# Delta-rule stage of a transformer kernel: two directions in lockstep, or as two streams eight steps apart

## The reference, cut to what matters

```python
def gdn_chunked(q, k, v, log_a, beta, s0):
    ...
    a_mat = jnp.where(strict, jnp.einsum('bhnid,bhnjd->bhnij', kb, k) * decay, 0.0) + jnp.eye(C, dtype=F32)
    rhs = jnp.concatenate([v * beta, kb * jnp.exp(g)[..., None]], axis=-1)
    sol = lax.linalg.triangular_solve(a_mat, rhs, left_side=True, lower=True)
    u, w = sol[..., :DV], sol[..., DV:]
    ...
    def step(s, xs):
        qk_c, qd_c, w_c, u_c, ke_c, ge_c = xs
        v_new = u_c - jnp.einsum('bhcd,bhdv->bhcv', w_c, s)
        o = jnp.einsum('bhcd,bhdv->bhcv', qd_c, s) + jnp.einsum('bhcs,bhsv->bhcv', qk_c, v_new)
        s = s * ge_c[..., None, None] + jnp.einsum('bhcd,bhcv->bhdv', ke_c, v_new)
        return s, o

def bidir_scan(scan_fn, ctx_f, ctx_b, lat_f, lat_b, s0):
    o_cf, s_f = scan_fn(*ctx_f, s0)
    o_cb, s_b = scan_fn(*flip_seq(ctx_b), s0)
    o_lf, _ = scan_fn(*lat_f, s_f)
    o_lb, _ = scan_fn(*flip_seq(lat_b), s_b)
    return o_lf + jnp.flip(o_lb, axis=2), (o_cf, o_cb)
```

## Time and profile before

| what | us |
|---|---|
| median of 3 runs (2361.44 to 2371.91) | 2362.75 |
| the profiled execution, its own time | 2375.91 |
| the profiled execution, span of the trace | 2373.9 |
| of it TensorE busy | 2099.6 (88%) |
| VectorE, ScalarE, GpSimd busy | 1189.2, 996.7, 134.1 |

### The profile page before, as it was taken

One profiled execution on the slowest core, in us unless ns is written; L12 is line 12 of the kernel. 1 busy time (PEld: TensorE's weight loads), 2 busy tenths in 40 slices (PEclk: granted clock), 3 DMA queues, 4 the chain that ended last, 5 costly groups with the idle time before them and its releaser, 6 DMA issues.

```text
span 2373.9 us, 41927 instructions
## 1 busy us (share of the span) xinstructions
PE 2099.6 (88%) x16886; PEld 1807.8 (76%) x16886; DVE 1189.2 (50%) x1933; ACT 996.7 (42%) x1636; POOL 134.1 (6%) x122
## 2 busy tenths in 40 slices
PE   5998788888899999898888979998689997798998
PEld 4783666686678778687777869997569997558997
DVE  4321566643543342454455257546546645655654
ACT  5332455613431242446222156445545545335553
POOL 0000000001000001001322110010000000000000
PEclk8999799858999999999999689999879998659999
DMA  9320466701233333234000036664325663204663
GB/s 288 91 77 6 141 178 189 203 1 45 71 98 89 90 97 91 80 99 124 4 4 4 1 92 187 179 186 122 89 71 157 186 179 101 70 1 119 188 178 118
DMA packets 490957, 254.62 MB, mean 107 GB/s; under 512 B 10816, under 2 KB 489664, under 8 KB 490688
## 3 DMA queue, kind: packets, MB, share of 16 engines
q1 hardware_dynamic: 490816, 252.59, 37.2%
HBM read 251.51 MB, written 1.05 MB: 106 GB/s over the span
## 4 chain that ended last, share of the span: by engine, by line
PE 75%; DVE 14%; ACT 7%; issue 3%; DMA 1%; SPq 0%; POOL 0%; ACTq 0%; DVEq 0%; POOLq 0%
PE bank L372 19%; PE bank L374 19%; PE bank L373 19%; DVE weights_lo L322 4%; PE bank L364 3%; ACT weights_hi L315 2%; PE bank L1835 2%; PE bank L921 1%; PE bank L1937 1%; PE bank L1149 1%; DVE att_small L968 1%; DMA ring<-ada_w 1%; PE bank L930 1%; PE bank L1851 1%; DVE a L2077 1%
## 5 line engine op out<-in xcount | busy, mean ns | idle before, releaser
L322 DVE TENSOR_TENSOR weights_lo<-ring,weights_hi 128x1024 fp32r<-128x1024 f32 x472 | 573.4, 1225 | 538.8 <-ACT weights_hi L315 535.8
L372 PE MATMUL bank<-x_hi,weights_hi 128*128 128x256 f32 (+1 forms) x2024 | 648.1, 320 | 71.0 <-DVE x_lo L400 29.0
L315 ACT ACTIVATE weights_hi<-ring 128x1024 fp32r<-128x1024 f32 x472 | 492.3, 1053 | 364.6 <-PE bank L374 327.0
L374 PE MATMUL bank<-x_hi,weights_lo 128*128 128x256 f32 (+1 forms) x2024 | 639.5, 316 | 0.0
L373 PE MATMUL bank<-x_lo,weights_hi 128*128 128x256 f32 (+1 forms) x2024 | 639.1, 316 | 0.0
L372 PEld LDWEIGHTS bank<-x_hi,weights_hi 128*128 128x128 f32 x2024 | 392.3, 194 | 104.8 <-issue 76.3
L373 PEld LDWEIGHTS bank<-x_lo,weights_hi 128*128 128x128 f32 x2024 | 392.1, 194 | 24.8 <-issue 1.2
L374 PEld LDWEIGHTS bank<-x_hi,weights_lo 128*128 128x128 f32 x2024 | 391.7, 194 | 24.4
L372 PE MATMUL bank<-hidden_hi,weights_hi 128*128 128x256 f32 (+1 forms) x864 | 272.8, 316 | 10.0 <-DVE hidden_lo L1401 6.8
L374 PE MATMUL bank<-hidden_hi,weights_lo 128*128 128x256 f32 (+1 forms) x864 | 272.9, 316 | 0.0
L373 PE MATMUL bank<-hidden_lo,weights_hi 128*128 128x256 f32 (+1 forms) x864 | 272.7, 316 | 0.0
(11 more groups left out here) (312 smaller groups left out, 2544.1 us busy)
## 6 DMA issues: line engine op xcount, KB each, us to landing
ring<-mlp_w SPq DMA_DIRECT2D x128, 512.0 KB, 4.0
ring<-ada_w SPq DMA_DIRECT2D x96, 512.0 KB, 4.9
ring<-w_ffn_in SPq DMA_DIRECT2D x88, 512.0 KB, 4.7
ring<-w_ffn_out SPq DMA_DIRECT2D x32, 512.0 KB, 3.7
ring<-gdn_w_in SPq DMA_DIRECT2D x24, 512.0 KB, 3.9
ring<-even_w_in SPq DMA_DIRECT2D x18, 512.0 KB, 4.5
ring<-w_out SPq DMA_DIRECT2D x16, 512.0 KB, 5.0
ring<-w_in_a SPq DMA_DIRECT2D x14, 512.0 KB, 3.8
```

The source lines that it names most:

```text
L315: nc.scalar.activation(w_hi[:, g % AHEAD, :], ring[:, g % RAW, :], ACT.Copy).then_inc(hi_done[g % AHEAD].sem, 1)
L322: nc.vector.tensor_tensor(w_lo[:, g % AHEAD, :], ring[:, g % RAW, :], w_hi[:, g % AHEAD, :].bitcast(F32), ALU.subtract).then_inc(lo_done[g ...
L372: pe.matmul(dst, lhs[0](k), rhs[0](k), start=start and k == 0, stop=False)
L374: last = pe.matmul(dst, lhs[1](k), rhs[0](k), start=False, stop=stop and k == nk - 1)
```

## The change

The stage is rewritten as 17 numbered steps per block and direction: 0 decay sums, 1 key products, 2 first blocks, 3 to 12 the five levels (odd: L, even: B), 13 values, 14 weights, 15 query products, 16 query decays (15 and 16 are empty for the context blocks). The recurrence of block p-1 is issued in steps 0, 1, 2 and 3 of block p (`ws`, `su`, `ws`, `su`). After block 3 come five more steps for its recurrence; the outputs are issued in step 4 of direction 1. All four engines walk the same double loop, in which direction 1 is eight steps behind:

The steps of TensorE, ScalarE and VectorE; no operation is added or dropped and none changes its shape:

```diff
-        def pe_gdn(pe):
-            pe_gdn_head(pe, 0)
-            for lv in range(LEVELS):
-                pe_gdn_q(pe, 0, lv)
-                pe_gdn_z(pe, 0, lv)
-            pe_gdn_tail(pe, 0)
-            for p in range(3):
-                pe_gdn_head(pe, p + 1)
...
+        def pe_gdn(pe):
+            def step(p, z, i):
+                if i == 0:
+                    if p < 4:
+                        decay_sums(p, z)
+                    if p >= 1:
+                        recur(p - 1, z, 0)
+                elif i == 1:
+                    if p < 4:
+                        key_products(p, z)
+                    if p >= 1:
+                        add_states(p - 1, z, 0)
+                elif i == 2:
+                    if p < 4:
+                        first_blocks(p, z)
+                    if p >= 1:
+                        recur(p - 1, z, 1)
+                elif i < 13 and i % 2:
+                    if p < 4:
+                        left(p, z, (i - 3) // 2)
+                    if i == 3 and 1 <= p < 4:
+                        add_states(p - 1, z, 1)
+                elif i < 13:
+                    if p < 4:
+                        both(p, z, (i - 4) // 2)
+                    if i == 4 and p >= 3 and z == 1:
+                        outputs(p - 1)
+                elif i == 13:
+                    values(p, z)
+                elif i == 14:
+                    weights(p, z)
+                elif p >= 2 and i == 15:
+                    query_products(p, z)
+                elif p >= 2:
+                    query_decays(p, z)
...
+                if i == 0:
+                    eyes(p, z)
+                elif i == 1:
+                    decay(p, z)
+                elif 3 <= i < 13 and i % 2:
+                    copy_left(p, z, (i - 3) // 2)
+                elif i == 13:
+                    copy_values(p, z)
+                elif i == 14:
+                    copy_weights(p, z)
+                elif i == 16 and p >= 2:
+                    query_decay(p, z)
...
+                if i == 0:
+                    if p < 4:
+                        decay_steps(p, z)
+                    if p >= 1:
+                        new_values(p - 1, z, 0)
+                elif i == 1:
+                    if p >= 1:
+                        new_states(p - 1, z, 0)
+                    if p < 4:
+                        below(p, z)
+                elif i == 2:
+                    if p < 4:
+                        first_blocks(p, z)
+                    if p >= 1:
+                        new_values(p - 1, z, 1)
+                elif i == 3 and 1 <= p < 4:
+                    new_states(p - 1, z, 1)
+                elif 4 <= i < 13 and i % 2 == 0:
+                    if p < 4:
+                        blocks(p, z, (i - 4) // 2)
+                    if i == 4 and p >= 3 and z == 1:
+                        outputs(p - 1)
+                elif i == 15 and p >= 2:
+                    query_products(p, z)
```

More of the change, by code:

```diff
@@ L1788, in tok, with chunk_at @@
             return slice(TBS[p][z] * P + c * C, TBS[p][z] * P + (c + 1) * C)
[L1790 to L1802, removed]
+        def chunk_at(z, st):
+            return st if z == 0 else 1 - st
@@ L1810, in pe_gdn_head, with key_products @@
                     .then_inc(N["g"], 1)
-            for z, u in units(p):
-                pe.wait_ge(N["d"], u + 1)
+            def key_products(p, z):
+                pe.wait_ge(N["d"], nth("d", z, p + 1))
                 for hp in range(4):
@@ L1818, in pe_gdn_head, with first_blocks @@
                 ins.then_inc(N["kk"], 1)
-            for z, u in units(p):
-                pe.wait_ge(N["aa"], u + 1)
+            def first_blocks(p, z):
+                pe.wait_ge(N["aa"], nth("aa", z, p + 1))
                 for c in range(2):
@@ L1828, in pe_gdn_head, with left @@
                 ins.then_inc(N["first"], 1)
-        def pe_gdn_q(pe, p, lv):
-            for z, u in units(p):
-                pe.wait_ge(N["xt"], nth(LEVELS + 1, p, lv, z))
+            def left(p, z, lv):
+                pe.wait_ge(N["xt"], nth("xt", z, (LEVELS + 1) * p + lv + 1))
                 for hd in range(NH):
@@ L1837, in pe_gdn_q, with both @@
                 ins.then_inc(N["q"], 1)
[L1839 to L1842, removed]
+            def both(p, z, lv):
+                pe.wait_ge(N["qc"], nth("qc", z, LEVELS * p + lv + 1))
+                pe.wait_ge(N["xx"], nth("xx", z, LEVELS * p + lv + 1))
                 for hd in range(NH):
@@ L1870, in pe_gdn_tail @@
                 ins.then_inc(N["wt"], 1)
[L1871 to L1893, removed]
+            def query_products(p, z):
+                pe.wait_ge(N["wtc"], nth("wtc", z, p + 1))
+                for hp in range(4):
+                    for c in range(2):
+                        for par in range(2):
+                            t = tok(p, z, c)
+                            ins = pe.matmul(four((bank_a(z), bank_b(z))[par])[half(c), hp, :], kf[half(par), hp, t],
+                                            qf[half(par), hp, t], start=True, stop=True)
+                ins.then_inc(N["qk"], 1)
@@ new lines, in query_decays, with recur @@
+            def query_decays(p, z):
+                pe.wait_ge(N["qkt"], nth("qkt", z, p - 1))
+                for hd in range(NH):
+                    col = la[:, TBS[p][z], z * NH + hd:z * NH + hd + 1].broadcast_to((P, C))
+                    ins = pe.matmul(bank_a(z)[half(hd % 2), (hd // 2) * P:(hd // 2 + 1) * P], col, upto[:, z, :],
+                                    start=True, stop=True)
+                ins.then_inc(N["g2"], 1)
+            def recur(p, z, st):
+                c, n = chunk_at(z, st), 2 * p + st
+                if n == 0:
+                    return
@@ L1916, in pe_gdn_su @@
                 ins.then_inc(N["su"], 1)
[L1918 to L1940, removed]
@@ L2002, in act_gdn_tail, with copy_weights @@
                 ins.then_inc(N["uc"], 1)
-            for z, u in units(p):
-                act.wait_ge(N["wt"], u + 1)
+            def copy_weights(p, z):
+                act.wait_ge(N["wt"], nth("wt", z, p + 1))
                 for c in range(2):
@@ L2021, in dve_gdn_head, with query_decay, dve_gdn, step @@
-        def dve_gdn_head(dve, p):
-            for z, u in units(p):
-                dve.wait_ge(N["g"], u + 1)
+            def query_decay(p, z):
+                act.wait_ge(N["g2"], nth("g2", z, p - 1))
+                nc.scalar.activation(qdc[:, z], four(bank_a(z), P), ACT.Exp).then_inc(N["qe"], 1)
+            gdn_steps(step)
+        def dve_gdn(dve):
+            def step(p, z, i):
+                if i == 0:
[22 more added lines that the diff above has]
+                    query_products(p, z)
+            def decay_steps(p, z):
+                dve.wait_ge(N["g"], nth("g", z, p + 1))
```

348 lines of the change are left out of this document (170 added, 178 removed).

## The result

The changed kernel is slower: 2385.56 us, median of 5 (2377.53 to 2399.05), against 2365.09 for before in the same session (median of 5). The ratio is 1.0087, 95% interval 1.0047 to 1.0126, or +20 us. I forecast 2369, and 2350 to 2383 as the range.

The account below looks back on a forecast made before the run. TensorE was taken to bound the kernel. Stretch terms -2.9, -0.4, -3.9, +0.6, 0, +11.3, 0 sum to +4.7; with 2 for supply +6.7, say 6, on the median 2362.75: 2369 us, range 2350 to 2383.

Parts of the forecast that it names:

- The bound: Whole kernel: TensorE is three quarters of the chain of waits; in the 247.7 us stage a better order could remove 40.7.
- Half a period: Hand layout of one direction's head beside the other's last levels and tail: 23.8 us, 25.2 with queries, idle 5.9 per half.
- block 1: Second block of the stage: 45.8 us against 46.2 before, so -0.4.
- Block 0: First block: direction 0 alone for 8 steps, 20.0 us, other half 20.8; 40.8 against 43.7, so -2.9.
- TensorE's clock: If the lone 34 us ran at low clock, its TensorE work would grow by up to 8 us; kept in the range.
- From the first to the second outputs: Direction 1 finishes levels, tail and recurrence without a partner: 34.2 us against 22.9, so +11.3.
- The outputs, set at 0 twice: First and second outputs keep their 20.3 and 23.1 us, with no idle to fill: 0 change each.
- the sign that I had named as not foreseen: Outputs at full clock, near half of 20.3 us, would be a thing the prediction did not foresee.
- Supply: Instruction fetches holding up TensorE in the stage: bounded between nothing and 6.6 us, taken as 2.
- The slower side: Case of supply holes, plus low clock in the end adding to the +11.3 us; chance 0.27.
- Supply holes on the chain: Rival: fetch holes of 0.94 us in X's first levels and where Y has left; +18, 2381 us; slower side's chance 0.27.
- the streams fill each other: Rival: nearly all TensorE idle in the stage closes except where one stream is alone; -14, 2349 us, chance 0.15.

Follow-up runs that it names:

- two other traces of before: The kernel before: once with no edit, 2363.19 us, and once with 512 independent 64 x 64 products added behind the second outputs, one run, no total time given.
- the fourth: The changed kernel plus extra float32 products, result unused, in TensorE's waits in the eight lone steps at start and at end; ratio to before 1.0018 (0.9997 to 1.0040).
- lag 4: The changed kernel with one number changed, direction 1 four steps behind instead of eight; ratio to the kernel before 1.0067 (1.0044 to 1.0090).
- sixth: The kernel before plus extra products: three after each head's key products, one and two in the last recurrence; 2348.63 us against 2365.13, ratio 0.9920.
- the burst: The kernel before plus 16 pieces of 32 independent 64 x 64 products behind the second outputs, no waits, one run; these records took 28.4 us.
- lag 3: The changed kernel with direction 1 three steps behind, extra products in the lone steps at start and end; 2361.48 us, ratio to before 0.9996 (0.9966 to 1.0026).
- the best reordered version: The changed kernel with no lag, one extra product in each of the first two heads and four in the last recurrence; 2346.19 us, ratio to before 0.9922.

## Why the prediction was wrong, by its own steps

**The bound.** "Three quarters of it is TensorE", and 40.7 us at most to win in the stage: this stood. TensorE's busy time in the stage is 209.8 against 207.05; in the two other traces of before it is 195.8 and 195.9, at a granted clock of 0.91 for 0.87 and 0.85.

**Half a period.** Forecast 23.8, and 25.2 with queries. Blocks 2 and 3 measured 48.5 (forecast 49.0) and 39.2 (39.2). The reading that idle is spread, not filled, is confirmed by FB's waits, 14.5 us in eight. The lengths fit better than their parts: the layout has TensorE idle for 11.8 of block 2's 49.0, the trace for 8.9 of 48.5, with the rest busy. So the close match is in part luck. In block 1 I had 45.8 for 48.0; 1.1 of that comes back in the fourth (46.9, granted clock 0.96 for 0.93).

**Block 0, the first wrong term.** I priced the lone eight steps at 20.0, with only the head at the lower clock. They took 25.5 at 0.50. At 0.93 they take 20.9, even with the hold-up by the extra products, so the layout was long enough and the clock was the error: 5.5 us. I had named it ("TensorE's clock", up to 8 us, "I keep that in the range") and left it out of the sum. Even the 8 was low: one L goes from 0.95 to 1.99, so 17 us of work could have grown by as much again. The other half of the block was 23.7, my 20.8 too short by 2.9, and 23.4 in the fourth. The granted clock is 0.83 and 0.85 in these two, so the extra products did not keep it there; how much of the 2.9 is the clock was not tried.

**From the first to the second outputs, the second wrong term, by the same error.** Forecast 34.2, measured 40.6 at a granted clock of 0.80. At 1.00 it is 38.6 with the extra products and, by the estimate in the fourth experiment, 35.2 without their hold-up. So the layout was 1.0 short and the clock 5.4. The mechanism ("the last eight steps have no partner") was right; the step that failed is that both lone stretches, but for the first head, were priced at TensorE's full clock, and the term for a lower one was put at nothing. In the one trace the clock's 5.5 and 5.4 make 10.9 of the 14.5 us between my +6 and the +20.5 of the medians; what blocks 0 and 1 were too short by otherwise, 2.9 and 2.2, comes next.

**The outputs, set at 0 twice, the third.** "They have no idle to fill" was read from rows at 0.56 and 0.51, and I took 20.3 and 23.1 as their length. They are 12 and 13 us at the full clock. In the three traces of before, either can be at the low clock or lose the full one on the way; behind the lone stretch the second began at 0.50 in the one trace of the changed kernel, and with lag 4 too (23.3 in both). Kept at the end, the clock made it 12.9, most of what moved the ratio from 1.0087 to 1.0039. The first went the other way, -8.2: it was the sign that I had named as not foreseen, outputs "at full clock". Against the mean of the three traces of before, 36.3 for both outputs, the changed 35.4 is a difference of -0.9: 0 for both together was not far off, but by luck.

**What the lag does at equal clock.** I took -7.2 for blocks 0 to 2 and +11.9 from block 3 to the second outputs. With the clock kept in both kernels (fourth against sixth) it is +2.6 (the heads of both hold some hold-up of their own) and +18.5, some 15 without the hold-up. The gain in the blocks was a gain over rows of before at 0.89 to 0.96: with its clock kept, before has 137.0 in these blocks instead of 142.8, and against that my own 135.6 for the changed kernel is a gain of 1.4. It measured 139.6.

**Supply.** The +2 was not there: waits on nothing fell to 0.3 us. The 4.7 us per fetch that I worked out was enough. The slower side had two parts. "Supply holes on the chain" is wrong, although its 2381 is the nearest number; the burst shows its premise true and its place wrong. The other part, the low clock in the end, is what came. The rule in the Trainium skill ("Runtime: NRT & Kernel Launch", Instruction fetch mechanics) that crossing a block is mostly hidden holds in the changed stage (0.3 us) and fails in the burst, where 1.4 to 2.5 us show at a boundary.

**The rival "the streams fill each other"** fell with block 1 and with FB's waits.

**The other rule that now bears on it.** The Trainium skill ("TensorE: Matmul & The Clock Gate", Part 1) says that the throttled state is the default and activity releases it. The rows agree: with products put in its waits, the granted clock of the lone part went from 0.50 to 0.93, of the stage from 0.85 to 0.97.

Open: what in the second half of block 0 I missed; whether the blocks at lag 3 shrink to those of lag 8 when their clock is kept too; and whether the lag of 8 with another place for the outputs would pay. None of these was tried.

## What to carry to other kernels

Running two dependent chains out of phase fills waits only as far as each engine's list lets it, and it always adds a start and an end in which one chain is alone. Price those ends at the low clock, and price too the work that comes behind them, since it starts at the clock they leave. Keep the clock in both kernels before saying what an order costs: here both had lost to it, by 19 and 16 us. An extra product is free only where nothing is ready behind it; on the chain it costs its length. Look at the granted clock of each stretch before taking its length as its cost: here, fifteen products put into the waits of an unchanged order gave 0.8%, as much as the best reordered version had with them, and the reordering alone gave nothing.

## What the runs showed of the hardware that was not expected

- The same 96 records of output products take 11.9 us at a granted clock of 1.00 and 19.8 to 20.3 at 0.56 to 0.57, 12.9 and 23.3 in the second place, at 1.00 and 0.50. The second outputs took 12.9 or 13.0 in all six traces of versions with extra products ahead of them. The first took 11.9 to 12.7 in five of these six and 20.1 in one. In the three traces of before the first lost the full clock on the way in two and kept it in one (12.2), and the second kept it in one (13.0).
- TensorE with nothing to wait for took 256 instructions of 64 x 64 products in 2.09 us and then stood for 1.4 to 2.5 us (once 0.48), at one instruction fetch per 3.5 to 4.6 us.
- Two executions of one program differ by 14 us in one stage (247.7 and 233.3), 10.6 of it in two pieces whose work is the same and whose granted clock is not; a single pair of traces gave +13.2 for a change whose medians differ by 20.
